# Two transformer blocks in fp32 on one core: sums ahead of the modulation, tables in two loads, reordered gates, half-column sums, compression in four column groups

## The chip, the cores and the metric

One core of one Trainium2 chip runs the whole program. The metric is the device time of one execution in microseconds (us), taken as the median of the runs. Engines: TensorE (PE for matmuls, PEld for its weight loads), VectorE (DVE), ScalarE (ACT), GpSimd (POOL), SyncE (SP, which here only issues transfers).

## What is computed

A sequence of 256 tokens with 1024 features passes through a first block of two layers and a second block of two layers, all in fp32. The reference, cut to what the change touches:

```python
c_act = silu(c)
for i in range(2):                              # first block
    mods = (c_act @ ada_w[i] + ada_b[i])        # 9 x 1024: shift, scale, gate for three sublayers
    h = rmsnorm(x) * (1 + scale) + shift;  x = x + 0.5 * gate * swiglu(h)
    h = ...;                               x = x + gate * (mla, then rwkv7)(h)
    h = ...;                               x = x + 0.5 * gate * swiglu(h)
x = rmsnorm(x)
# second block, layer 0: mixer_ab (dilated attention | convolution + mlstm), layer norm, MoE, layer norm
#   mlstm: gates i, f from the input projection; log_sigmoid(f), cumulative sums, stabilised exponentials
# layer 1: mixer_c, layer norm, MoE, layer norm
def compress(t, pos, w1, w2):                   # 15 windows of 32 tokens, two groups: 30 rows of 4096
    flat = (t[:, cidx] + pos).reshape(..., 32 * 128)
    return gelu(flat @ w1) @ w2                 # w1: 4096 x 256
```

## The kernel before

Activations lie transposed (`xT`: 128 partitions x 8 tiles x 256 tokens). The phases run in the order `ffn0, mla, ffn1, ffn2, rwkv, ffn3, final, ab, moe0, c, moe1`. Each engine has one hand-written instruction list, and semaphores tie the lists together. What an engine does in what order is thus fixed by the place of the call in its own list.

Weights come through a ring of four slots of 2 MB (`ring`), which SyncE fills in the order of `STREAM`; a load waits until the piece four places earlier is given back (`freed`: by VectorE's `dve_free` for modulation and feed-forward pieces, by `slot_free` or `mh_used` for others). In the feed-forwards and the projections of `mla`, `ab` and `c`, a weight is split into a rounded high part (ScalarE: `up_high`, `mix_high`) and a low rest (VectorE: `up_low`, `mix_low`), and each product is three matmuls. `mix_high(g)` and `mix_low(g)` work on half pieces; in `ab` the halves 4 and 5 are the first piece after the two raw ones, 14 to 17 the output weights, in `c` 10 to 13 are the output weights.

**The modulation** (`ada`): 36 pieces of 512 columns. For one piece VectorE multiplies the eight row tiles of the weight by the eight columns of `cact` and adds them up in a chain (`ada_step`, L1876 and L1879, buffer `z` in `work`); TensorE then sums over the partitions with four matmuls whose weights are 128 columns of `z` and whose moving operand is one column of ones (`ada_sum`, L568); VectorE adds the bias into `mods` (`ada_finish`, L1895). Pieces 0 to 3 stand at the very start, before the norm of `ffn0`; the other 32 are spread over the feed-forwards (12, 8, 10, 2), in `ADA_STEPS`. In `ffn0` the norm follows: squares by ScalarE (L1418), column sums by TensorE (`norm_sums`, L548), the root (L1420), the reciprocal (L1943), the scaled tiles (L1953), their high and low parts (L1440, L1950). `hold(6, 7)` issues seven matmuls without use (L541) ahead of the first dense ones, and `up_low` (L1915) must be done for the first tile (L585 are the products).

**Tables.** ScalarE's queue loads at the start `vec`, the whole of `const` (128 x 4673 columns: identity, ones, masks, rotations and so on) and `xT` (L1369 to L1371); TensorE, VectorE and ScalarE wait for `const_in`.

**Mixer `ab`.** TensorE projects with split halves in the order of pieces 3, 4, 5, 6, 0, 1, 2 (`split_piece` L655, `split_tokens` L668), with the two gate columns between them (`by_token`, L1068). VectorE runs low parts, the convolution (`conv`, L2354 and L2356), the gates (L2365, L2366, which TensorE awaits as `lin_fed` for the cumulative sums at L1090), the stabilised exponentials and the normalisation of the linear part, then two low parts, the addition of the mask to the bias table (L2458) and the attention (`maxima` L2088, first thing of each head). The bias table is written to DRAM and read back by ScalarE's queue (`load_bias`, L1638).

**Mixer `c`.** The compression on TensorE (L1323): for keys and for values 32 matmuls over 32 token offsets, weights 128 x 30 (the 30 window rows), moving 128 x 256, all accumulated in 30 partitions of one bank; every fp32 matmul shows as two instructions. ScalarE copies the 30 rows (L1826), TensorE turns them (L1330), ScalarE applies gelu (L1832), TensorE multiplies by `w2`, ScalarE copies (L1835, L1836), and the attention starts. The copies of halves 10 and 11 stand in ScalarE's list between its two copies of raw rows.

## Time and profile before

| | us |
|---|---|
| median of 3 runs (lowest, highest) | 2578.42 (2578.35, 2588.62) |
| profiled execution, own time | 2581.79 |
| its span, first to last instruction | 2580.0 |
| PE busy | 2429.1 (94%) |
| DVE busy | 1709.2 (66%) |
| ACT busy | 1101.5 (43%) |
| POOL busy | 81.4 (3%) |
| mean granted clock of TensorE | 0.964 of 2.4 GHz |

Busy shares are means over phases of different kinds. The chain of waits follows the program back from its last instruction and tells which engine the end hangs on at each time; the timeline gives each instruction with the idle time before it and what ended that. A matmul's own duration includes its way through the array, so rates of matmuls are read from the distance of starts, or from the length of a group divided by its count. "PEclk" is the granted clock: 1.00 is 2.4 GHz, 0.50 is 1.2 GHz.

### The profile page before, as it was taken

To read this page: it belongs to the slowest core of one execution; us is meant where nothing else is said; L and a number is where in the kernel's file an instruction comes from. 1 tells how busy PE (TensorE), PEld (TensorE's weight loads), DVE (VectorE), ACT (ScalarE), POOL (GpSimd) and SP (SyncE) were. 2 spreads that over 40 slices of the span, in tenths; PEclk is the share of its full clock that TensorE was granted. 3 is DMA by queue.
4 is the path that set the end of the run, shared out by engine and by line. 5 is a ranking of instruction groups with operands and counts; after the bars stand their busy time and mean duration, and the time that the engine had idled before them with its cause. 6 is when DMAs were issued, how large, how long until landed. Compare 5 with 4: busy or idle time off the path is not lost.

```text
span 2580.0 us, 40749 instructions
## 1 busy us (share of the span) xinstructions
PE 2429.1 (94%) x17382; PEld 2136.8 (83%) x17382; DVE 1709.2 (66%) x2365; ACT 1101.5 (43%) x1375; POOL 81.4 (3%) x116
## 2 busy tenths in 40 slices
PE   3999989999999998889999989999999989999998
PEld 3999748999999777779999868788888858788886
DVE  5987566876886455655555665548895375557985
ACT  2333254334333033433334443447774252546773
POOL 0000000000000003630000000000000000000000
PEclk9999989999999998889999978999999989999999
DMA  7887304774876230004554503549984400747991
GB/s 294 326 312 270 123 25 158 288 282 154 310 285 256 98 123 26 3 2 185 201 194 124 180 26 126 227 171 354 367 324 185 169 35 21 290 188 304 368 362 49
DMA packets 48284, 502.10 MB, mean 195 GB/s; under 512 B 4968, under 2 KB 9448, under 8 KB 10856
## 3 DMA queue, kind: packets, MB, share of 16 engines
q1 hardware_dynamic: 42480, 490.52, 50.2%
q10 hardware_dynamic: 5624, 8.97, 1.4%
q8 instruction: 138, 2.26, 0.3%
q14 instruction: 42, 0.34, 0.1%
HBM read 496.33 MB, written 3.15 MB: 194 GB/s over the span
## 4 chain that ended last, share of the span: by engine, by line
PE 82%; DVE 11%; ACT 3%; DMA 2%; issue 2%; POOL 1%; ACTq 0%; DVEq 0%; POOLq 0%
PE PS L1229 25%; PE PS L585 25%; PE PS L655 7%; PE PS L631 4%; PE PS L548 2%; DMA ring<-stream 1%; PE PS L668 1%; PE PS L1323 1%; PE PS L568 1%; DVE work L1879 1%; DMA xT<-x_in 1%; PE PS L964 1%; PE PS L767 1%; PE PS L1280 1%; DVE w_up_lo L1915 1%
## 5 line engine op out<-in xcount | busy, mean ns | idle before, releaser
L585 PE MATMUL PS<-x_part_hi,w_up_hi 128*128 128x256 f32 x1408 | 404.4, 287 | 9.4 <-DVE x_part_lo L1950 6.5
L585 PE MATMUL PS<-x_part_lo,w_up_hi 128*128 128x256 f32 x1408 | 399.4, 284 | 0.0
L585 PE MATMUL PS<-x_part_hi,w_up_lo 128*128 128x256 f32 x1408 | 399.3, 284 | 0.0
L2489 DVE TENSOR_TENSOR ring_low<-ring,m_w_up 128x2048 fp32r<-128x2048 f32 x128 | 293.1, 2291 | 134.0 <-ACT m_w_up L1727 134.0
L1727 ACT ACTIVATE m_w_up<-ring 128x2048 fp32r<-128x2048 f32 x128 | 245.3, 1917 | 187.5 <-PE PS L1229 187.5
L585 PEld LDWEIGHTS PS<-x_part_hi,w_up_hi 128*128 128x128 f32 x1408 | 271.0, 193 | 12.7 <-issue 8.0
L585 PEld LDWEIGHTS PS<-x_part_lo,w_up_hi 128*128 128x128 f32 x1408 | 271.3, 193 | 0.0
L585 PEld LDWEIGHTS PS<-x_part_hi,w_up_lo 128*128 128x128 f32 x1408 | 271.1, 193 | 0.0
L1229 PE MATMUL PS<-m_w_up,xg_hi 128*128 128x512 f32 x640 | 253.0, 395 | 3.8 <-DVE work L2503 3.8
L1229 PE MATMUL PS<-ring_low,xg_hi 128*128 128x512 f32 x640 | 254.2, 397 | 0.0
L1229 PE MATMUL PS<-m_w_up,xg_lo 128*128 128x512 f32 x640 | 253.2, 396 | 0.0
L1915 DVE TENSOR_TENSOR w_up_lo<-ring,w_up_hi 128x2048 fp32r<-128x2048 f32 x88 | 201.3, 2289 | 17.7 <-ACT w_up_hi L1386 17.5
L585 PE MATMUL PS<-hid_hi,w_down_hi 128*128 128x256 f32 x704 | 199.3, 283 | 0.0
L585 PE MATMUL PS<-hid_lo,w_down_hi 128*128 128x256 f32 x704 | 199.2, 283 | 0.0
L585 PE MATMUL PS<-hid_hi,w_down_lo 128*128 128x256 f32 x704 | 199.2, 283 | 0.0
L1879 DVE SCALAR_TENSOR_TENSOR work<-ring,cact,work 128x512 f32<-128x512 f32 x252 | 189.0, 750 | 6.9
L1455 ACT ACTIVATE w_down_hi<-ring 128x1024 fp32r<-128x1024 f32 x88 | 93.1, 1058 | 199.6 <-PE PS L585 199.6
L1386 ACT ACTIVATE w_up_hi<-ring 128x2048 fp32r<-128x2048 f32 x88 | 167.1, 1902 | 12.5 <-DMA ring<-stream 12.5
L1229 PEld LDWEIGHTS PS<-m_w_up,xg_hi 128*128 128x128 f32 x640 | 121.0, 189 | 32.7 <-DVE work L2503 4.7
L2047 DVE TENSOR_TENSOR w_down_lo<-ring,w_down_hi 128x1024 fp32r<-128x1024 f32 x88 | 107.5, 1221 | 59.3 <-ACT w_down_hi L1455 58.2
L1450 ACT ACTIVATE work<-PS 128x256 f32<-128x256 f32 x88 | 33.8, 384 | 262.3 <-PE PS L585 262.2
L1229 PEld LDWEIGHTS PS<-m_w_up,xg_lo 128*128 128x128 f32 x640 | 121.0, 189 | 28.6
(523 smaller groups left out, 5158.8 us busy)
## 6 DMA issues: line engine op xcount, KB each, us to landing
ring<-stream SPq DMA_DIRECT2D x133, 2048.0 KB, 7.8
ring<-stream SPq DMA_DIRECT2D x88, 1536.0 KB, 6.7
work<-stream SPq DMA_DIRECT2D x48, 1024.0 KB, 8.3
hT<-stream SPq DMA_DIRECT2D x16, 1024.0 KB, 7.5
ring<-stream SPq DMA_DIRECT2D x3, 1152.0 KB, 5.6
const<-const_tables ACTq DMA_DIRECT2D x1, 2336.5 KB, 18.7
bias_scratch<-work ACTq DMA_DIRECT2D x1, 2048.0 KB
work<-bias_scratch ACTq DMA_DIRECT2D x2, 1024.0 KB, 7.5
```

The lines of the kernel that those rows point to most:

```text
L548: last = mm(bank(7, T, at), ones, ap, start=(i == 0), stop=(i == len(parts) - 1))
L585: last = mm(out, w[a][:, lo:lo + P], x[b][:, at:at + T], start=start and i == 0, stop=stop and i == 2, skip_group_check=skip)
L631: last = mm(bank(m // 2, T, (m % 2) * T, 0, rows), piece_cols(name, k, lo + j * P, rows, width), rhs[:, k, :], start=(k == 0), stop=(k == ...
L655: last = mm(bank(m // 2, T, (m % 2) * T, 0, rows), w[a][:, k, j * step:(j + 1) * step], x[b][:, k * T:(k + 1) * T], start=first[j] and (pa ...
L1229: last = mm(out, x[b], w[a], start=start and i == 0, stop=stop and i == 2)
L1386: fn(w_up[j % 2][0][:, :], piece(f"{tag}.{j}")[:, 0:2048], ACT.Copy).then_inc(S("up_rounded"), 1)
L1455: fn(w_down[j % 2][0][:, :], piece(f"{tag}.{j}")[:, 2048:3072], ACT.Copy).then_inc(S("down_rounded"), 1)
L1727: fn(m_w_up[g % 3][:, :], piece(f"mu{l}.{q}")[:, h * 2048:(h + 1) * 2048], ACT.Copy).then_inc(S("up_rounded"), 1)
L1879: ins = stt(z, w, cact[:, k:k + 1], z, ALU.mult, ALU.add)
L1915: tt_(lo[:, :], piece(f"{tag}.{j}")[:, 0:2048], hi[:, :].bitcast(F32), ALU.subtract).then_inc(S("up_split"), 1)
L2047: tt_(lo[:, :], piece(f"{tag}.{j}")[:, 2048:3072], hi[:, :].bitcast(F32), ALU.subtract).then_inc(dve_free, 1)
L2489: tt_(ring_low[n][:, part], ring[n][:, part], m_w_up[g % 3][:, :].bitcast(F32), ALU.subtract).then_inc(S("up_split"), 1)
```

## The change

1. Head. `norm_sums` now comes before the modulation on TensorE, and VectorE takes the reciprocal between pieces 2 and 3. For pieces 0 to 3, two of the eight row tiles (`ADA_DIRECT = 2`) are multiplied by TensorE straight from the ring (eight matmuls with one moving column), and VectorE's chain has six steps instead of eight; both go into one sum. VectorE gives piece p's slot back only when it has done piece p+1's steps and read piece p's result. `up_low` of tile 0 moves behind the third scaled tile.
2. Tables. `const` is loaded as 264 columns at the start (identity, ones, eps) and the other 4409 in ScalarE's list at tile 6 of `ffn0`; `mla` and GpSimd's `rwkv` wait for that.
3. Modulation sums of the 32 later pieces by halves: each of four matmuls becomes two with 64-column weights, whose results go to partitions 0 to 63 and 64 to 127.
4. `ab`: VectorE's order of low parts 4 and 5, gates and convolution; the bias load, its mask addition and low part 14 earlier, low part 15 inside the attention.
5. `c`: the matmul of offset i goes to the 32-partition group i mod 4, with 32 weight columns (two of them foreign); the copy takes 128 partitions; the turning is a matmul with a folding matrix (four stacked identities) that also adds the four groups. ScalarE's copy of half 11 moves behind the gelu.

```diff
@@ constants and the second load
+CONST_HEAD = 2 * P + 8
-            act.dma_start(const[:, :], const_d[:, :]).then_inc(S("const_in"), 16)
+            act.dma_start(const[:, 0:CONST_HEAD], const_d[:, 0:CONST_HEAD]).then_inc(S("const_in"), 16)
...
                 for j in range(n + 1):
+                    if tag == "ffn0" and j == 6:
+                        act.dma_start(const[:, CONST_HEAD:], const_d[:, CONST_HEAD:]).then_inc(S("const_in"), 16)
@@ ada_sum on TensorE
                 for m in range(4):
-                    last = mm(bank(b + p % 2, 4)[:, m:m + 1], z[:, m * P:(m + 1) * P], ones[:, 0:1], start=True,
-                              stop=True)
+                    for lo in (0, 64):
+                        last = mm(bank(b + p % 2, 4, 0, lo, lo + 64)[:, m:m + 1], z[:, m * P + lo:m * P + lo + 64],
+                                  ones[:, 0:1], start=True, stop=True)
@@ TensorE, pieces 0 to 3, now behind norm_sums("ffn0")
+            def ada_head():
+                pe.wait_ge(S("cact_ready"), 1)
+                for p in range(ADA_HEAD):
+                    take(f"ada.{p}")
+                    if p >= 2:
+                        pe.wait_ge(S("ada_read"), p - 1)
+                    out = bank(4 + p % 2, 4)
+                    for k in range(KT - ADA_DIRECT, KT):
+                        for m in range(4):
+                            mm(out[:, m:m + 1], piece_cols(f"ada.{p}", k, m * P, P), cact[:, k:k + 1],
+                               start=(k == KT - ADA_DIRECT and m == 0), stop=False, skip_group_check=True)
+                    pe.wait_ge(S("ada_part"), p + 1)
+                    z = W(SW_ADA + 512 * (p % ADA_BUFS), 512)
+                    for m in range(4):
+                        last = mm(out[:, m:m + 1], z[:, m * P:(m + 1) * P], ones[:, 0:1], start=False, stop=True,
+                                  skip_group_check=True)
+                    last.then_inc(S("ada_sum"), 1)
+                pe.wait_ge(S("ada_read"), ADA_HEAD)
@@ VectorE, pieces 0 to 3
+            def ada_head():
+                for p in range(ADA_HEAD):
+                    for k in range(KT - ADA_DIRECT):
+                        ada_step(p, k)
+                    if p > 0:
+                        ada_finish(p - 1)
+                        dve.sem_inc(dve_free, 1)
+                    if p == 2:
+                        dve.wait_ge(S("const_in"), 32)
+                        line.next("std_ready")
+                        done(v.reciprocal(RSTD, STD))
+                ada_finish(ADA_HEAD - 1)
+                dve.sem_inc(dve_free, 1)
@@ ab on VectorE
-                dve.wait_ge(S("ab_copied"), 1)
-                mix_lows("ab", 4, 5)
-                conv(0, 4)
+                mix_lows("ab", 4)
                 line.next("softlog_ready")
...
                 done(tt_(lf, lf, sl[:, :, 4:8], ALU.subtract), "lin_fed")
+                mix_lows("ab", 5)
+                dve.wait_ge(S("ab_copied"), 1)
+                conv(0, 4)
...
                 hh = ls(4352, 1024)
+                dve.wait_ge(S("bias_in"), 32)
+                bm = W(A_BM, 8 * ATT).rearrange("p (h c) -> p h c", c=ATT)
+                done(tt_(bm, bm, C("dilated").unsqueeze(1).broadcast_to([P, 8, ATT]), ALU.add))
+                mix_lows("ab", 14)
                 line.next("lnum_copied")
...
-                mix_lows("ab", 14, 15)
-                dve.wait_ge(S("bias_in"), 32)
-                bm = W(A_BM, 8 * ATT).rearrange("p (h c) -> p h c", c=ATT)
-                done(tt_(bm, bm, C("dilated").unsqueeze(1).broadcast_to([P, 8, ATT]), ALU.add))
-                attention("ab", {4: [linear_out], 5: [lambda: mix_lows("ab", 16)], 6: [linear_low]})
+                attention("ab", {4: [linear_out], 5: [lambda: mix_lows("ab", 16)], 6: [linear_low], 2: [lambda: mix_lows("ab", 15)]})
@@ ab on ScalarE: the bias load now behind the copies of halves 10 and 11
                 mix_highs("ab", 10, 11)
+                act.wait_ge(S("bias_stored"), 16)
+                load_bias(A_BM)
@@ c on TensorE
-                            last = mm(bank(4 + 2 * kv, T, T, 0, 2 * NCMP), b3[:, 16 * half + i, :],
-                                      piece(name)[:, i * T:(i + 1) * T], start=(half == 0 and i == 0),
-                                      stop=(half == 1 and i == 15))
+                            at, lo = 2 * NCMP * (16 * half + i), 32 * (i % 4)
+                            n = 32 if at + 32 <= 960 else 2 * NCMP
+                            last = mm(bank(4 + 2 * kv, T, T, lo, lo + n), b3[:, at:at + n],
+                                      piece(name)[:, i * T:(i + 1) * T], start=(half == 0 and i < 4),
+                                      stop=(half == 1 and i >= 12), skip_group_check=True)
...
-                        last = nc.tensor.transpose(bank(4 + 2 * kv + m, 2 * NCMP),
-                                                   W(C_RAW + kv * T + m * P, P, 0, 2 * NCMP),
-                                                   ident[0:2 * NCMP, 0:2 * NCMP])
+                        last = mm(bank(4 + 2 * kv + m, 2 * NCMP), W(C_RAW + kv * T + m * P, P), W(C_FOLD, 2 * NCMP),
+                                  start=True, stop=True)
@@ c on ScalarE
                     if kv == 0:
-                        mix_highs("c", 10, 11)
+                        mix_highs("c", 10)
...
                 last.then_inc(S("hid_gelu"), 1)
+                mix_highs("c", 11)
```

How the instructions stand now. First, the start of TensorE's list: the sums of squares (`hT`), the modulation's matmuls and the warm-up (`const` alone). Before:

```order
L568 MATMUL PS<-const,work 128x1 x16
L548 MATMUL PS<-hT,const 128x256 x8
L541 MATMUL PS<-const 128x256 x7
L585 MATMUL PS<-x_part_hi,w_up_hi 128x256
L585 MATMUL PS<-x_part_lo,w_up_hi 128x256
```

Now:

```order
L551 MATMUL PS<-hT,const 128x256 x8
L586 MATMUL PS<-cact,ring 128x1 x8
L591 MATMUL PS<-const,work 128x1 x4
L586 MATMUL PS<-cact,ring 128x1 x8
L591 MATMUL PS<-const,work 128x1 x4
L586 MATMUL PS<-cact,ring 128x1 x8
L591 MATMUL PS<-const,work 128x1 x4
L586 MATMUL PS<-cact,ring 128x1 x8
L591 MATMUL PS<-const,work 128x1 x4
L544 MATMUL PS<-const 128x256 x7
```

The sums stand first, each piece has twelve narrow matmuls instead of four, and only the warm-up is left between the last of them and the dense ones.

Second, VectorE in `ab` around the gates (two rows of 128x8, L2365 and L2366 before, L2397 and L2398 now; `ring_low` rows are low parts, the 128x256 rows the convolution). Before:

```order
L1922 TENSOR_TENSOR ring_low_49<-ring,half_high_87 128x8x256
L1922 TENSOR_TENSOR ring_low_49<-ring,down_low_85 128x8x256
L2354 TENSOR_SCALAR work<-work,vec 128x256 x4
L2356 SCALAR_TENSOR_TENSOR work<-work,vec 128x256 x12
L2365 TENSOR_SCALAR work<-work 128x8
L2366 TENSOR_TENSOR work<-work 128x8
```

Now:

```order
L1955 TENSOR_TENSOR ring_low_49<-ring,half_high_87 128x8x256
L2397 TENSOR_SCALAR work<-work 128x8
L2398 TENSOR_TENSOR work<-work 128x8
L1955 TENSOR_TENSOR ring_low_49<-ring,down_low_85 128x8x256
L2388 TENSOR_SCALAR work<-work,vec 128x256 x4
L2390 SCALAR_TENSOR_TENSOR work<-work,vec 128x256 x12
```

The gates no longer stand behind one low part and half of the convolution.

Third, VectorE at the end of the linear part of `ab`, before the first head of the attention (L2088 before, L2122 now, 128x384). Before:

```order
L2442 TENSOR_TENSOR work<-work 128x1024
L1922 TENSOR_TENSOR ring_low_50<-ring,down_low_85 128x8x256
L1922 TENSOR_TENSOR ring_low_50<-ring,half_high_86 128x8x256
L2458 TENSOR_TENSOR work<-work,const 128x3072
L2088 SCALAR_TENSOR_TENSOR work<-PS,work 128x384
```

Now, the two places to which they moved, with the rows between left out:

```order
L2448 TENSOR_REDUCE work<-work 128x8
L2452 TENSOR_TENSOR work<-work,const 128x3072
L1955 TENSOR_TENSOR ring_low_50<-ring,down_low_85 128x8x256
L2456 TENSOR_SCALAR work<-work 128x8
...
L2481 TENSOR_TENSOR work<-work 128x1024
L2122 SCALAR_TENSOR_TENSOR work<-PS,work 128x384
```

The mask addition and one low part now precede the wait for the linear numerator (L2456), and the attention follows the linear part directly; the other low part stands after the third head's scores.

## Rows read from the trace of the kernel before

**Rows 1.** The page, part 4: shares of the span in the chain of waits.
```profile
PE 82%; DVE 11%; ACT 3%; DMA 2%; issue 2%; POOL 1%; ACTq 0%; DVEq 0%; POOLq 0%
```

**Rows 2.** Timeline, 0 to 56 us: start us, us, engine, line, operation, [idle before <-releaser].
```profile
10.26 5.47 DVE L1879 SCALAR_TENSOR_TENSOR work<-ring,cact,work 128x512 f32<-128x512 f32 x7
...
27.29 3.57 PE L568 MATMUL PS<-const,work 128*128 128x1 f32 x16 [27.29 <-DMA xT<-x_in]
...
43.64 5.66 PE L548 MATMUL PS<-hT,const 128*128 128x256 f32 x16 [0.25 <-DVE mods L1895]
...
49.14 3.19 PE L541 MATMUL PS<-const 128*128 128x256 f32 x14
...
49.92 1.75 DVE L1943 RECIPROCAL small<-small 128x256 f32<-128x256 f32 x1 [6.14 <-ACT small L1420]
...
55.61 0.55 PE L585 MATMUL PS<-x_part_hi,w_up_hi 128*128 128x256 f32 x1 [3.29 <-DVE x_part_lo L1950]
```

**Rows 3.** TensorE's waits in the `ab` mixer, 1383 to 1570 us: total, times, longest.
```profile
PE PS L701 <- DVE work L2090: 8.8, 1, 8.8
...
PE PS L1090 <- DVE work L2366: 5.4, 1, 5.4
```

**Rows 4.** Timeline of the `c` mixer, 2036 to 2092 us, three engines.
```profile
2041.24 29.35 PE L1323 MATMUL PS<-ring,work 128*30 128x256 f32 x128
...
2064.34 3.71 ACT L1395 ACTIVATE half_high<-ring 128x2048 fp32r<-128x2048 f32 x2 [7.15 <-DMA ring<-stream]
...
2070.63 0.37 ACT L1826 ACTIVATE work<-PS 30x256 f32<-30x256 f32 x1 [2.58 <-PE PS L1323]
...
2076.06 0.19 DVE L2088 SCALAR_TENSOR_TENSOR work<-PS,work 128x30 f32<-128x30 f32 x1 [5.19 <-PE PS L699]
```

**Rows 5.** Windows: us, length, busy (count) of PE, PEld, DVE, ACT, POOL, PEclk, DMA, GB/s.
```profile
20.00:25.00 5.00, 0.00 (x0) 0.00 (x0) 4.75 (x8) 0.00 (x0) 0.00 (x0) 1.00 0.99 421
55.00:60.00 5.00, 4.39 (x20) 4.42 (x21) 5.00 (x13) 3.03 (x7) 0.00 (x0) 0.50 0.01 3
100.00:110.00 10.00, 10.00 (x86) 10.00 (x85) 9.42 (x15) 3.36 (x3) 0.00 (x0) 1.00 0.89 335
```

**Rows 6.** DMA issues: KB each, median us from issue to landing.
```profile
ring<-stream SPq DMA_DIRECT2D x88, 1536.0 KB, 6.7
...
const<-const_tables ACTq DMA_DIRECT2D x1, 2336.5 KB, 18.7
...
xT<-x_in ACTq DMA_DIRECT2D x1, 1024.0 KB, 25.6
```

**Rows 7.** The chain of waits in order of time, 0 to 130 us.
```profile
101.38 0.79 PE PS L568 x8
```

**Rows 8.** TensorE's timeline behind a dense stretch of the `ab` mixer.
```profile
1406.60 1.85 PE L1068 MATMUL PS<-ring,xT 128*128 128x8 f32 x16
...
1408.69 2.86 PE L1068 MATMUL PS<-ring,xT 128*128 128x8 f32 x16
```

**Rows 9.** ScalarE's timeline in the first feed-forward.
```profile
104.92 1.92 ACT L1386 ACTIVATE w_up_hi<-ring 128x2048 fp32r<-128x2048 f32 x1 [2.45 <-DMA ring<-stream]
```

**Rows 10.** TensorE's timeline in the `rwkv` mixer: matmuls with 64-column weights.
```profile
1021.91 1.15 PE L981 MATMUL PS<-work 128*64 128x64 f32 x32
...
1024.76 0.39 PE L1017 MATMUL PS<-work 128*64 128x128 f32 x4
...
1024.98 0.39 PE L1021 MATMUL PS<-work 128*64 128x128 f32 x4
```

**Rows 11.** VectorE's timeline in the `ab` mixer, 1418 to 1512 us.
```profile
1421.92 2.29 DVE L1922 TENSOR_TENSOR ring_low<-ring,down_low 128x2048 fp32r<-128x2048 f32 x1 [9.87 <-ACT down_low L1395]
...
1490.36 0.17 DVE L2417 TENSOR_SCALAR work<-work 128x8 f32<-128x8 f32 x1 [4.33 <-ACT work L1700]
...
1506.07 3.35 DVE L2458 TENSOR_TENSOR work<-work,const 128x3072 f32<-128x3072 f32 x1
...
1509.45 0.56 DVE L2088 SCALAR_TENSOR_TENSOR work<-PS,work 128x384 f32<-128x384 f32 x1
```

62 lines of the change are left out of this document (30 added, 32 removed).

## Prediction

> **What bounds the kernel now.** The chain of waits comes first: TensorE carries 82% of it and VectorE 11% [rows 1], so a change pays only where TensorE stands still, runs at half clock, or does fewer cycles. The timeline then shows three such places. At the head, TensorE does its first matmul at 27.29 us and its first dense product at 55.61 [rows 2]; between them lie the modulation's four pieces (each seven chained VectorE steps, 5.47 us, after a first one), the sums of squares (5.66), a warm-up (3.19) and the reciprocal (1.75). In the `ab` mixer TensorE's waits name two stops on VectorE, 5.4 and 8.8 us [rows 3]. In the `c` mixer one line of 128 half-instructions takes 29.35 us with weights of 30 columns [rows 4]. Elsewhere dense products follow each other, and only fewer or cheaper instructions count there.
>
> **Head: what the new order gives.** All early loads share the engines: 421 GB/s at 20 to 25 us [rows 5]. The tables and x go out from ScalarE's queue and land 18.7 and 25.6 us after issue [rows 6], x at 27.3. The table load shrinks from 2336 KB to 132, so 2.26 MB less lie ahead of x: at 421 GB/s that is 5.4 us, x lands at 21.9. ScalarE squares it, and the sums start at 22.9 and end at 28.6 (5.66 us, partly cold [rows 2]). Piece 0 on TensorE is now 8 narrow products straight from the weights and 4 from VectorE's partial sum, 24 instructions where there were 8. Cold, 16 took 3.57 us, 0.22 each [rows 2]; warm, 8 took 0.79, 0.10 each [rows 7]. After a dense stretch 16 narrow ones still took 1.85 us (warm) and only the next 16 2.86 [rows 8], so piece 0 is warm: 2.4 us, until 31.0. VectorE has by then done pieces 0 and 1 (six steps of 0.78, 4.7 us, instead of eight) and stands at piece 0's result; this is a new wait, and the loads behind it wait too, since the ring's first slot is now given back at 31.2, not near 16. Then piece 2 until 35.7, result and reciprocal until 37.5, piece 3 until 42.2. TensorE has done piece 3's direct part by then; the last four products, cold, take 1.8: 44.0. The old order had the modulation at 43.6, so nothing is won up to here. What is won stands behind it: sums, root, reciprocal and the first weight subtraction no longer follow. Fourteen warm-up matmuls from cold take 5.2 us (5.66 less two warm ones of 0.23 [rows 2]) and hide the subtraction: dense work starts at 49.3, not 55.6, and warm, where it ran at a clock of 0.50 before [rows 5]. VectorE's eight scaled tiles and the second subtraction then hold TensorE's second tile until 56.1 where it was 63.1. Gain **7.0 us**. The first two weight pieces, requested at 31.2 and 35.8, land 6.7 us later [rows 6] and are rounded by 44.4, just in time; the ring is full at about 54, and its next slot comes free only at 58.5. If TensorE is cold for all of it, 4 us come back; if x lands early enough for VectorE alone to set the pace, 4 more are won: 3 to 11.
>
> **The rest of the tables** (2.26 MB) now goes out in the first feed-forward after tile 5. There transfers are busy for 0.89 of the time at 335 GB/s [rows 5], and ScalarE already waits 2.45 us for a piece [rows 9] while TensorE never idles. At that rate the load takes 6.7 us and shares the engines with the pieces. The wait shown says that the margin is small. Bounds: nothing if the free tenth and the ring's stock absorb it, 6.7 if nothing does. I take **+3.0**.
>
> **Modulation sums by halves.** Behind the head 32 pieces pay 0.79 us each [rows 7] on the chain. Now a set is 16 instructions with 64-column weights, in alternating halves. The nearest row: 32 instructions with 64-column weights and 64 columns moving took 1.15 us, 0.036 each [rows 10], so a set takes 0.58, 0.21 less; 32 of them 6.7. Twelve lie in the first feed-forward, where data is short, and count half: **5.5 us**. Bounds: 0.025 each (a quarter of the 0.10, full overlap) gives 10; 0.05 each (half of it, no overlap) gives nothing, and a little lost at each switch +2.
>
> **The gates' order in `ab`.** VectorE does the two small gate operations before the convolution and a weight subtraction (2.29 [rows 11]), so TensorE's wait of 5.4 us goes. With it goes the cold stretch behind it, worth 2.7 us (dense products at half speed for some 5.4 us, as begins at 55.61 [rows 5]): 8.1 in all. What is late next is the 8.8 us wait. VectorE's bias addition (3.35) and two subtractions stand ahead of its first score at 1509.45, starting at 1501.7: 7.8 us that go. The addition and one subtraction (5.6) move up to where VectorE idled 4.33 us [rows 11]; the bias load moves up on ScalarE's queue and should land before. That costs 1.7. The other subtraction (2.2) goes into the attention, in which VectorE sets the pace. Sum: 8.1 + 7.8 - 1.7 - 2.2 = **12.0 us**; 9 if upstream gains are partly covered by the wait for weights, 14.5 if the shorter stop keeps the clock up.
>
> **Compression in four groups.** The 128 instructions take 0.229 each with 256 columns moving [rows 4]. Now neighbours write four different 32-row groups. That groups overlap is in the trace: with two 64-column groups 4 instructions of 128 columns start every 0.22 us, 0.055 each [rows 10], half of 128 x 0.229/256 = 0.115. I take full overlap, 0.057. The first two weight pieces then take 5.1 us (cold for the first 3) instead of 14.6. But ScalarE's half of the output weights stands between the two results and needs a slot that the second piece frees: before, freed at 2055.9 (half of the 29.35 behind 2041.24) and landed at 2064.3 [rows 4], 8.4 us; now freed at 2046.3, landed at 2054.7. One copy (1.86), then the second result at 2056.6, where before it was 2070.6. From there 5.5 us to VectorE's first score, plus 0.7 because copy and subtraction of half 11 now lie behind it: 2062.8, not 2076.06. Gain **13.3 us**, not the 22 that TensorE alone would save: the rest turns into a wait on that transfer. The four copies that build the folding matrix and the folding itself (8 instructions for 4) cost under 0.5 us in VectorE's idle time and in the 5.5. Bounds: 15 if the transfer is faster, 9.6 if only two groups overlap, -1 if none.
>
> A rule speaks against this part. In the Trainium skill, "TensorE: Matmul & The Clock Gate", section "The mechanism", a weight load overlaps with running matmuls only when the row group differs; here all groups use all 128 rows. By the letter of it the four groups would be serial, which is the first rival. The trace disagrees for two groups (0.055 against 0.115), so I follow the trace.
>
> **Sum.** -7.0 + 3.0 - 5.5 - 12.0 - 13.3 = -34.8 us. The profiled execution took 2581.8 us, so 2547.0 for it; the median of the runs lies 3.4 lower, at 2578.4, and so does the forecast: **2543.6 us**. A measurement of this kernel can tell some 0.5%, 13 us, from no change.
>
> **Rivals.**
> A, the column groups are serial: the compression gives -1 instead of 13.3, 2543.6 + 14.3 = 2557.9. For it: no row has four groups. Against: [rows 10]. 8%.
> B, the first feed-forward is bound by its transfers: the second table load costs its 6.7 (3.7 more than summed) and the halves' gain in that stage is lost (1.3): 2548.6, and with the head's gain lost too, because slots came free 15 us later, 2555.6. For it [rows 5, 9]; against, the transfers stood idle at 55 to 60 us (3 GB/s, [rows 5]), so stock is not short there. 10%.
> C, TensorE stays cold through the whole head, 24 instructions of 0.22 for piece 0 and sums that take 1.1 longer: 4 us, 2547.6. 8%, inside the range.
> D, slower: the narrow half-column sets cost the clock. If the granted clock fell to 1.2 GHz behind each of the 32 sets, the dense products after it would lose 2.7 us each, as behind a stop now: 86 us. With the halves' 5.5 gone, -29.3 + 86 = +57, 2635. It decides from 11 sets on (29.3/2.7). For it: narrow matmuls did lower the clock in [rows 8]. Against: that took over 3 us of them, these sets last under 1 us, and behind today's sets the clock stays at 1.00 [rows 5]. 2%.
> E, the edits do their parts but new waits eat most of it (the bias load late, or VectorE late in `ab`): 2560 to 2580. 3%.
> The forecast itself has 69%.
>
> **Numbers.** The range is 2532 to 2557: the good ends of two or three terms on one side, B and C whole on the other; A, D and E stay out. Faster by over 0.5% (under 2565.5) 0.94, within 0.5% 0.04, slower 0.02.
>
> **What would show it.** Head: VectorE idle some 11 us before its first result, first dense product at 49 to 50 us. Tables: ScalarE waits for pieces right behind the load. Sets of 16 in under 0.6 us. In `ab`, no wait of TensorE for the gates, and its last one under 3 us. In `c`, TensorE done with the compression near 2050 on the old scale and ScalarE waiting for a transfer before the second result. It is wrong if the first dense product comes after 54 us, if the compression's instructions start 0.2 us apart, or if a clock of 0.50 shows in the feed-forwards.

## The result, and the profile after

The changed kernel takes 2546.57 us (median of 4 runs, 2541.78 to 2549.04) against 2578.66 for the kernel before (4 runs on the same chip, 2578.35 to 2588.62). The ratio is 0.9864, with a 95% interval of 0.9836 to 0.9892: 32.1 us less, where the prediction had 34.8, and its 2543.6 us is 3.0 below the median. The pair of profiled executions differs by more, 2581.79 to 2541.78 or 40.0 us. The lengths of the stages show where.

The page of the changed kernel, parts 1, 4 and 5 (line engine op, out<-in, shapes, count | busy, mean ns | idle before, releaser). L604 was L585 before, L1409 was L1386, L1948 was L1915:

```profile
PE 2406.5 (95%) x17706; PEld 2121.7 (84%) x17706; DVE 1703.5 (67%) x2361; ACT 1101.2 (43%) x1375; POOL 81.3 (3%) x116
...
PE 78%; DVE 12%; DMA 4%; ACT 3%; issue 2%; POOL 1%; ACTq 0%; DVEq 0%; POOLq 0%
...
L604 PE MATMUL PS<-x_part_hi,w_up_hi 128*128 128x256 f32 x1408 | 404.2, 287 | 8.9 <-DVE w_up_lo L1948 5.4
...
L1409 ACT ACTIVATE w_up_hi<-ring 128x2048 fp32r<-128x2048 f32 x88 | 167.3, 1903 | 34.9 <-DMA ring<-stream 34.7
```

TensorE's share of the chain fell from 82% [rows 1] to 78%, and transfers doubled theirs to 4%. ScalarE's waits for ring pieces grew from 12.5 us to 34.7: the kernel now waits for data where it waited for arithmetic.

The norm's sums (L551, L548 before) open every stage, and the chain of waits gives their times. Their starts in the changed kernel, behind the head's own:

```profile
257.16 3.71 PE PS L551 x16
411.35 3.47 PE PS L551 x16
617.56 3.71 PE PS L551 x16
824.65 3.47 PE PS L551 x16
1173.89 3.64 PE PS L551 x16
1375.53 3.69 PE PS L551 x16
1535.94 3.47 PE PS L551 x16
...
1934.50 3.47 PE PS L551 x16
...
2120.32 3.47 PE PS L551 x16
...
2518.67 3.47 PE PS L551 x16
```

The differences of neighbours are the stages' lengths; the same view of the kernel before gives the other column. "Predicted" sorts the prediction's terms by stage (12 of the 32 sets lie in the first feed-forward, 20 in the others).

| stage | before | after | gain | predicted |
|---|---|---|---|---|
| head and first feed-forward | 261.48 | 257.16 | 4.3 | 5.3 |
| `mla` | 155.73 | 154.19 | 1.5 | 0 |
| other three feed-forwards | 616.97 | 614.94 | 2.0 | 4.2 |
| `rwkv` | 350.77 | 349.24 | 1.5 | 0 |
| `ab` | 176.52 | 160.41 | 16.1 | 12.0 |
| `moe0` | 403.39 | 398.56 | 4.8 | 0 |
| `c` | 195.30 | 185.82 | 9.5 | 13.3 |
| `moe1` | 398.54 | 398.35 | 0.2 | 0 |

Four stages that no edit reaches gained 8.1 us. `moe0` shows what that is. In 14 profiled executions of 14 programs it took 398.4 to 404.9 us although its instructions never changed, and the other stages scatter likewise. This is the row of its first stretch in the kernel before, and then in the changed one (us, length, busy of PE, PEld, DVE, ACT, POOL with counts, granted clock, DMA share, GB/s):

```profile
1561.50:1624.00 62.50, 56.48 (x274) 47.76 (x273) 42.14 (x93) 27.32 (x33) 0.00 (x0) 0.86 0.47 188
```

```profile
1536.00:1595.60 59.60, 53.32 (x274) 44.83 (x272) 42.09 (x93) 27.30 (x33) 0.00 (x0) 0.91 0.50 198
```

The same 274 matmuls take 2.9 us more at a mean granted clock of 0.86 than at 0.91. Across the 14 executions `moe0`'s mean granted clock is 0.99 in the shortest and 0.97 in the longest. Such episodes of the lower level (1.2 instead of 2.4 GHz) differ between executions, and they can account for a profiled pair that differs by 40 where the medians differ by 32. Stage lengths are therefore compared only where an edit acts and where rows inside show the cause.

**The head** (TensorE, VectorE, ScalarE's rounding copies and the sync queue, changed kernel; "..." marks rows left out):

```profile
22.91 6.29 PE L551 MATMUL PS<-hT,const 128*128 128x256 f32 x16 [22.91 <-ACT hT L1441]
...
29.03 1.84 PE L586 MATMUL PS<-cact,ring 128*128 128x1 f32 x16
...
31.68 3.56 PE L586 MATMUL PS<-cact,ring 128*128 128x1 f32 x16
31.93 0.16 DVE L1920 TENSOR_TENSOR mods<-PS,vec 128x4 f32<-128x4 f32 x1 [12.96 <-PE PS L591]
32.00 15.60 SPq L482 DMA_DIRECT2D ring<-stream  x4
...
38.36 1.91 ACT L1409 ACTIVATE w_up_hi<-ring 128x2048 fp32r<-128x2048 f32 x1 [8.66 <-DMA ring<-stream]
...
47.22 0.16 DVE L1920 TENSOR_TENSOR mods<-PS,vec 128x4 f32<-128x4 f32 x1 [3.56 <-PE PS L591]
47.43 5.55 PE L544 MATMUL PS<-const 128*128 128x256 f32 x14 [0.25 <-DVE mods L1920]
...
56.70 2.29 DVE L1948 TENSOR_TENSOR w_up_lo<-ring,w_up_hi 128x2048 fp32r<-128x2048 f32 x1
```

The sums start at 22.91 (predicted 22.9), and VectorE idles 12.96 us before its first result ("some 11"). The first slot comes free at 32.00. Piece 0's 16 narrow instructions take 1.84 us; from piece 1 on 16 take 3.56: the clock had fallen. With the 8 instructions of the partial sum that is 5.1 us a piece, more than the 4.6 that VectorE needs for six steps and a result. The modulation is done at 47.4 instead of 44.0, and the first dense product comes at 52.6 instead of 49.3.

**`ab`.** The chain's fourth block of input products, in the kernel before and in the changed one:

```profile
1447.28 11.36 PE PS L655 x96
```

```profile
1429.52 11.35 PE PS L674 x96
```

Counted from the stage's first sums (1384.95 and 1375.53) it starts at 62.33 and 53.99, 8.3 us earlier. TensorE's waits of 5.4 and 8.8 us [rows 3] are both gone from its list; the longest left are 1.8 and 2.8, both inside the attention (at 1485.9 and 1493.4). VectorE's small gate operation now stands at 1406.26, the bias addition (3.36) at 1468.30, and the first score is read at:

```profile
1406.26 0.17 DVE L2398 TENSOR_TENSOR work<-work 128x8 f32<-128x8 f32 x1
...
1484.67 0.56 DVE L2122 SCALAR_TENSOR_TENSOR work<-PS,work 128x384 f32<-128x384 f32 x1
```

**`c`.** TensorE, ScalarE and VectorE, changed kernel:

```profile
2011.58 6.91 PE L1344 MATMUL PS<-ring,work 128*32 128x256 f32 x96
...
2020.83 3.00 PE L1344 MATMUL PS<-ring,work 128*32 128x256 f32 x32 [2.35 <-DMA ring<-stream]
2027.64 1.91 ACT L1418 ACTIVATE half_high<-ring 128x2048 fp32r<-128x2048 f32 x1 [10.42 <-DMA ring<-stream]
2029.46 0.36 ACT L1851 ACTIVATE work<-PS 128x256 f32<-128x256 f32 x1
...
2036.19 0.19 DVE L2122 SCALAR_TENSOR_TENSOR work<-PS,work 128x30 f32<-128x30 f32 x1 [0.48 <-PE PS L718]
```

What took 29.35 us [rows 4] takes 12.2, of which 2.35 are a wait for the fourth weight piece. The transfer for ScalarE's half lands at 2027.64 and holds the second result until 2029.46, as foretold.

### The profile page after: what moved, and what is told of

Its sections match the earlier page's. It is cut to its first block, busy times and chain, and to the rows that moved or that the text cites. A ratio compares the mean times of both kernels' runs of the same rounds, so it can differ in the third digit from the quotient of the medians.

```text
span 2540.0 us, 41400 instructions
## 1 busy us (share of the span) xinstructions
PE 2406.5 (95%) x17706; PEld 2121.7 (84%) x17706; DVE 1703.5 (67%) x2361; ACT 1101.2 (43%) x1375; POOL 81.3 (3%) x116
## 4 chain that ended last, share of the span: by engine, by line
PE 78%; DVE 12%; DMA 4%; ACT 3%; issue 2%; POOL 1%; ACTq 0%; DVEq 0%; POOLq 0%
PE PS L1248 25%; PE PS L604 23%; PE PS L674 7%; PE PS L650 4%; DMA ring<-stream 3%; PE PS L551 2%; DVE work L1908 1%; PE PS L983 1%; PE PS L687 1%; DVE w_up_lo L1948 1%; PE PS L786 1%; DMA xT<-x_in 1%; PE PS L1299 1%; PE PS L748 1%; PE PS L992 1%
## 5 line engine op out<-in xcount | busy, mean ns | idle before, releaser
L604 PE MATMUL PS<-x_part_hi,w_up_hi 128*128 128x256 f32 x1408 | 404.2, 287 | 8.9 <-DVE w_up_lo L1948 5.4
L604 PE MATMUL PS<-x_part_hi,w_up_lo 128*128 128x256 f32 x1408 | 398.3, 283 | 0.0
L604 PE MATMUL PS<-x_part_lo,w_up_hi 128*128 128x256 f32 x1408 | 398.2, 283 | 0.0
L604 PEld LDWEIGHTS PS<-x_part_hi,w_up_hi 128*128 128x128 f32 x1408 | 269.6, 191 | 12.9 <-DVE w_up_lo L1948 7.7
L604 PEld LDWEIGHTS PS<-x_part_lo,w_up_hi 128*128 128x128 f32 x1408 | 269.9, 192 | 0.0
L604 PEld LDWEIGHTS PS<-x_part_hi,w_up_lo 128*128 128x128 f32 x1408 | 269.9, 192 | 0.0
L1948 DVE TENSOR_TENSOR w_up_lo<-ring,w_up_hi 128x2048 fp32r<-128x2048 f32 x88 | 201.2, 2288 | 19.0 <-ACT w_up_hi L1409 18.9
L604 PE MATMUL PS<-hid_hi,w_down_hi 128*128 128x256 f32 x704 | 199.3, 283 | 0.0
L604 PE MATMUL PS<-hid_lo,w_down_hi 128*128 128x256 f32 x704 | 199.2, 283 | 0.0
L604 PE MATMUL PS<-hid_hi,w_down_lo 128*128 128x256 f32 x704 | 199.1, 283 | 0.0
L1908 DVE SCALAR_TENSOR_TENSOR work<-ring,cact,work 128x512 f32<-128x512 f32 x244 | 183.0, 750 | 6.6
L1409 ACT ACTIVATE w_up_hi<-ring 128x2048 fp32r<-128x2048 f32 x88 | 167.3, 1903 | 34.9 <-DMA ring<-stream 34.7
L1248 PEld LDWEIGHTS PS<-ring_low,xg_hi 128*128 128x128 f32 x640 | 120.1, 188 | 27.3
```

The source lines that it names most:

```text
L604: last = mm(out, w[a][:, lo:lo + P], x[b][:, at:at + T], start=start and i == 0, stop=stop and i == 2, skip_group_check=skip)
L1248: last = mm(out, x[b], w[a], start=start and i == 0, stop=stop and i == 2)
L1409: fn(w_up[j % 2][0][:, :], piece(f"{tag}.{j}")[:, 0:2048], ACT.Copy).then_inc(S("up_rounded"), 1)
L1908: ins = stt(z, w, cact[:, k:k + 1], z, ALU.mult, ALU.add)
L1948: tt_(lo[:, :], piece(f"{tag}.{j}")[:, 0:2048], hi[:, :].bitcast(F32), ALU.subtract).then_inc(S("up_split"), 1)
```

## The experiments

Each is the changed kernel with one edit, or with several where the text says so; "+" and "-" are against it, and "..." marks what is left out. Ratios are to the kernel before, timed beside it. The runs come from several chips, so two experiments are compared by their ratios and intervals first. Lengths of stages are from one profiled execution each.

**Full-width sets.**

```diff
-  for lo in (0, 64):
-      last = mm(bank(.., lo, lo + 64)[:, m:m + 1], z[:, m * P + lo:m * P + lo + 64], ones[:, 0:1], ...)
+  last = mm(bank(b + p % 2, 4)[:, m:m + 1], z[:, m * P:(m + 1) * P], ones[:, 0:1], ...)
```

> The changed kernel with its 32 modulation sums behind the head at full width again (8 instructions a set). Theory of the prediction: a set costs 0.79 us instead of 0.58, so the second to fourth feed-forward (20 sets) end 4.2 us later against the stage before, and the run is 5.5 us slower than the changed kernel. Rival, from the changed kernel's trace, where those three stages gained 2.0 us in all: the switch of column groups takes half of it back, 0.10 us a set, so 2.0 us there and 3 in all. In the first feed-forward nothing, if transfers bound it.

Measured: 2553.64 us, ratio 0.9900 [0.9877, 0.9922]. The chain of waits in the second feed-forward repeats a double tile with one set. This kernel:

```profile
494.37 17.38 PE PS L603 x144
512.54 17.38 PE PS L603 x144
```

and the changed one:

```profile
489.21 17.46 PE PS L604 x144
507.24 17.46 PE PS L604 x144
```

The period is 18.17 and 18.03: 0.14 us a set, between the two theories. The set itself shrank by 0.22 (18.17 - 17.38 = 0.79, 18.03 - 17.46 = 0.57), as the prediction had it, but 0.08 comes back in the dense products around it: the first narrow instruction starts 0.21 us behind the last dense one, whose neighbours start 0.12 apart (a full-width set follows after 0.12 too). Over 32 sets 4.5 us. The medians differ by 7.1, but stages without a set scatter by more than the rest: `moe1` took 405.0 us in this profiled execution and 398.4 in the changed kernel's. A property listed in the Trainium skill, "TensorEngine Tiling (Array Packing)", section "Key Properties", says that changing the tiling mode drains the engine; the extra 0.09 us fits that, though no run here separates a drain from another cause.

**Half-column sets, one group after the other.**

```diff
-  for m in range(4):
-      for lo in (0, 64):
+  for lo in (0, 64):
+      for m in range(4):
```

> The changed kernel with the 16 half-column instructions of each modulation set in another order: first the four of rows 0 to 63, then the four of rows 64 to 127, instead of alternating. In the changed kernel a set takes 0.56 us (0.035 each) and the double tile of the feed-forward with its set 18.03 us, against 18.17 with full-width sets. Theory: what makes a half-column instruction cheap is that its weight load runs beside the other column group's work, so with one switch in place of seven a set costs 0.8 us or more and the period is 18.2 or more. Rival: the price is that of the 64 columns alone (half the weights to load), order does not matter, and the period stays at 18.03.

Measured: 2557.88 us, ratio 0.9901 [0.9881, 0.9920]. Its chain:

```profile
473.99 17.46 PE PS L604 x144
492.27 17.46 PE PS L604 x144
```

Period 18.28, set 0.82 us: slower than full width. The theory holds: the alternation makes the halves cheap, not their width.

**The rest of the tables at tile 18.**

```diff
-  if tag == "ffn0" and j == 6:
+  if tag == "ffn0" and j == 18:
```

> The changed kernel with the second table load (2.2 MB) sent after tile 18 of the first feed-forward instead of tile 6, where no modulation piece is loaded any more. If the load costs what the prediction says, the end of the first feed-forward comes 3.0 us earlier (6.7 if it costs its whole transfer) and the long waits for ring pieces at 103 and 121 us shrink. Rival: the stage is short of data already because the first four slots come free late, the stall only moves to another piece, and the end moves by under 1 us.

Measured: 2547.84 us, ratio 0.9883 [0.9860, 0.9907], and the stage ended at 260.07, later than the 257.16 it should have beaten. Neither theory held. The head shows something else: the program is the same there, yet here piece 1's narrow products ran at the full clock too:

```profile
28.29 1.84 PE L586 MATMUL PS<-cact,ring 128*128 128x1 f32 x16
30.00 1.03 PE L591 MATMUL PS<-const,work 128*128 128x1 f32 x8
30.89 1.93 PE L586 MATMUL PS<-cact,ring 128*128 128x1 f32 x16
31.14 0.16 DVE L1920 TENSOR_TENSOR mods<-PS,vec 128x4 f32<-128x4 f32 x1 [12.26 <-PE PS L591]
```

The modulation was done at 44.3 and the first dense product came at 49.12, the prediction's own 44.0 and 49.3. In all eight executions with this order of the head piece 0 was warm and pieces 2 and 3 were cold. Piece 1 was warm in four of them (first dense product at 49.1 to 49.9) and cold in four (52.5 to 52.9). The windows from 32 to 34 us of the changed kernel and of the experiment on output halves below, which run the same program up to here:

```profile
32.00:34.00 2.00, 2.00 (x11) 2.00 (x11) 1.93 (x4) 0.00 (x0) 0.00 (x0) 0.50 0.60 111
```

```profile
32.00:34.00 2.00, 2.00 (x20) 2.00 (x20) 1.93 (x3) 0.00 (x0) 0.00 (x0) 1.00 0.81 190
```

Estimated from such rows, the clock fell at 31.2 to 32.0 us in the four late executions and at 32.8 to 34.0 in the four early ones. The Trainium skill, "TensorE: Matmul & The Clock Gate", section "What's actually happening", says that the count of cold matmuls at a kernel's start varies from run to run; these runs agree, with 3 us. Little of the 3 us reached the end of the stage: the four early executions ended it at 257.5 to 260.1, the four late ones at 257.2 to 262.0. TensorE's wait for weights in this stage came to 8.2 us here, and to 3.4 in the changed kernel (total, times, longest):

```profile
PE PS L604 <- DVE w_up_lo L1948: 8.2, 7, 2.2
```

```profile
PE PS L604 <- DVE w_up_lo L1948: 3.4, 4, 1.7
```

**The rest of the tables behind x.**

```diff
   act.dma_start(xT[:, :], x_d[:, :]).then_inc(S("const_in"), 16)
+  act.dma_start(const[:, CONST_HEAD:], const_d[:, CONST_HEAD:])...
...
-  if tag == "ffn0" and j == 6:
-      act.dma_start(const[:, CONST_HEAD:], ...)
```

> The changed kernel with the rest of the tables (2.2 MB) sent right behind x instead of in the first feed-forward after tile 6. Transfers stand idle between 22 us (x and the first four pieces have landed) and 32 us (the first slot comes free), so theory: the load is free there, x still lands at 22, the waits for ring pieces at 103 and 121 us (13.5 and 8.9 us of the chain) shrink to some 7 each, and the first feed-forward ends 3 to 6 us earlier than at 257.2, near 252.5. Rival: the load shares the engines with x and the pieces from the start, x lands 3 to 5 us later (25 to 27), and the head gives back what the stage wins: end at 255 to 258. Second rival, from the run with the tables at tile 18, whose stage ended 2.9 us later: the stage's stalls come from the four slots and not from the tables, and the end moves by under 1 us.

Measured: 2542.49 us, ratio 0.9864 [0.9834, 0.9895]. The sums start at 22.64, so x isn't held back, and between 22 and 30 us 437 GB/s move where the changed kernel moved 193:

```profile
22.00:30.00 8.00, 7.36 (x37) 6.50 (x37) 0.00 (x0) 2.52 (x5) 0.00 (x0) 1.00 1.03 437
```

The load is free there, and still the stage ends at 257.48: the second rival. TensorE waits 5.6 us for weights without the 2.2 MB in the stage; with them it waited 3.4, 5.2, 5.4 and 7.7 us in four executions.

**No direct products in the head.**

```diff
-ADA_DIRECT = 2
+ADA_DIRECT = 0
```

> The changed kernel without direct products in the head: VectorE does all eight steps of each piece, TensorE 4 sums. If the cold narrow products of TensorE set the pace of the head (5.12 us a piece in the changed kernel), VectorE's 5.9 us a piece for the pieces 2 and 3 now does: piece 1's result at 29.9, modulation done near 44.5 to 46 where it was 47.2, so the head is 1 to 3 us faster although VectorE does more. Rival: VectorE set the pace, and two more steps on two pieces make it 3 us slower (50).

Measured: the modulation was done at 45.8, within the theory, so TensorE indeed set the pace of the changed head; the stage ended at 254.46. But the four runs spread from 2547.76 to 2557.66, median 2553.40, ratio 0.9906 [0.9880, 0.9931], slower than the changed kernel if anything. The profiled execution is the fastest of the four, and what held the others isn't in a trace. This stays open.

**Slots given back early.** Pieces 0 and 1 wholly on VectorE, pieces 2 and 3 as they were.

```diff
-ADA_DIRECT = 2
+ADA_DIRECT = (0, 0, 2, 2)
...
-  if p >= ADA_HEAD:
+  if p >= ADA_HEAD or ADA_DIRECT[p] == 0:
       dve.sem_inc(dve_free, 1)
```

> The changed kernel, but VectorE does all eight steps of pieces 0 and 1 and gives their ring slots back right behind them, as the kernel before did; pieces 2 and 3 keep their direct products. Theory from nine traces: behind the head the first feed-forward is bound by the four ring slots and ends 225 to 229 us after the first slot comes free (changed kernel: free at 32.0, end at 257.2), wherever the tables go and wherever the first dense product starts. Here the first slots come free near 15.6 and 21.5 and the first dense product stays at 51 to 53: the end must then be set by computing, 201 us behind the first dense product as in the run with both head edits, near 253, with under 1.5 us of TensorE waits for weights in the stage. Rival: the third and fourth slot decide, and the end stays at 256 to 258.

Measured: 2545.18 us, ratio 0.9866 [0.9832, 0.9899]. The first slot came free at 15.66, the first weight piece was rounded at 30.36 instead of 38.36, and the stage ended at 252.92 as expected. By another sum, though: the first dense product came at 47.69 and not at 51 to 53, and the end not 201 behind it but 205.2, with 4.1 us of waits for weights and not under 1.5. The earlier dense product isn't owed to the slots: with no direct products for pieces 0 and 1 the first result was read at 29.30 and the modulation was done at 42.3, and the warm-up follows that. What the slots gave is less clear. The waits of 4.1 us are below the 5.1 to 8.2 of the four executions with a dense start at 49.1 to 49.9, but in the range of all eight, and waits for ring pieces remain at 70, 94 and 116 us of the chain. "The end is 226 behind the first slot" is thus refuted as a rule (237 here).

**Pieces 0 and 1 ahead of the norm's sums.**

```diff
+  pe.wait_ge(S("cact_ready"), 1)
+  ada_head(0, 2)
   norm_sums(ph)
-  ada_head()
+  ada_head(2, ADA_HEAD)
```

> The changed kernel with the products of pieces 0 and 1 ahead of the norm's sums on TensorE (it stands idle until x lands at 22), and the reciprocal behind piece 3's steps on VectorE. If what holds the head is VectorE idle for 13 us behind piece 0's result, the modulation is done near 35 us instead of 47.2 and the first dense product starts near 41 instead of 52.6. If the first feed-forward were bound by computing, all 11 to 12 us would reach its end. Theory now: the stage is bound by its transfers behind the head (ring pieces waited for at 75, 103, 121, 149 us), and since slots come free 11 us earlier, the transfers start earlier too: 5 to 10 us at its end. Rival: the engines that move data are full anyway until 130 us, and under 3 us reach the end.

Measured: 2534.40 us, ratio 0.9830 [0.9807, 0.9854]. The median is 12 us under the changed kernel's and the ratio 0.34% lower (9 us), with intervals that overlap. The modulation is done at 40.3, the first dense product comes at 45.65, the stage ends at 250.49: 6.7 of the 7.0 us reach its end, inside the 5 to 10. This head also gives the first slot back at 23.84 instead of 32.00, so the run doesn't separate slots from the earlier dense start. The modulation came late against the hoped 35, because its input now waited for the small tables until 14.56. Another 4.6 us are `rwkv`'s (344.65 instead of 349.24), a stage no edit touches, at a higher granted clock; the runs don't show that they belong to this edit.

**More of the same.** Added to the kernel just told: the small tables on a semaphore of their own, the rest of the tables behind x as above, and the first weight subtraction ahead of the last result.

```diff
-  act.dma_start(const[:, 0:CONST_HEAD], ...).then_inc(S("vec_in"), 16)
+  act.dma_start(const[:, 0:CONST_HEAD], ...).then_inc(S("bias_stored"), 16)
...
+  up_low("ffn0", 0)
   ada_finish(ADA_HEAD - 1)
```

> The kernel with pieces 0 and 1 ahead of the norm's sums, and in addition: the modulation vector no longer waits for the small tables (they held it until 14.6 instead of 9.4), the rest of the tables goes out behind x, and the first weight subtraction stands ahead of VectorE's last modulation result instead of behind it. Theory: modulation done near 35 us instead of 40.3, first dense product near 40.5 instead of 45.7 (the 14 warm-up matmuls now set it), the end of the first feed-forward near 244 instead of 250.5. Rival: transfers hold x back (25 instead of 22), or the stage is bound by its slots and the end moves by under 3 us.

Measured: 2535.57 us, ratio 0.9837 [0.9804, 0.9869]. The stage ended at 249.00 where 244 was expected and 250.49 stood before, so the end moved by under 3 us, as the rival had it. But x wasn't held back, as that rival had it: it landed at 22.0. The sums start at 24.20 because ScalarE now loads its activation table (1.28 us) behind x, and so it does in the last experiment below, whose tables go out at tile 6. What came late is piece 3, at 31.96 (26.78 in that last experiment), and with it the modulation, at 41.3. The slots are free from 19.0 on, so the tables go out beside new pieces, and their load took 30.0 us where it took 12.8 in the last experiment:

```profile
31.96 0.48 DVE L1908 TENSOR_SCALAR work<-ring,cact 128x512 f32<-128x512 f32 x1 [5.56 <-DMA ring<-stream]
```

Dense work began 28 us behind the first slot, TensorE's waits for weights fell to 1.2 us, and the end came 201.7 behind the first dense product.

**Gate operations behind the convolution again.**

```diff
-  done(ts_(lf, ...)); done(tt_(lf, ...), "lin_fed")
   mix_lows("ab", 5)
   dve.wait_ge(S("ab_copied"), 1)
   conv(0, 4)
+  done(ts_(lf, ...)); done(tt_(lf, ...), "lin_fed")
```

> The changed kernel with the two small gate operations of the ab mixer behind the convolution again. The two traces put 8.3 us on this part (from the stage's norm sums to the fourth pair of product blocks). If the two small operations alone do that, TensorE waits 5.4 us for VectorE again, the blocks behind it run cold for 2.7 us, and the stage is 8.3 us longer (168.7 instead of 160.4). Rival: the bias addition that now stands in VectorE's idle time absorbs part of the delay, so 5.4 to 6.

Measured: 2560.62 us, ratio 0.9908 [0.9876, 0.9941]; `ab` took 169.83, 9.4 more than 160.41. The first score, counted from the stage's start, comes 8.5 us later, and the wait is back, as the expectation had it:

```profile
PE PS L1109 <- DVE work L2400: 5.4, 1, 5.4
```

**Compression in two groups.**

```diff
-  at, lo = 2 * NCMP * (16 * half + i), 32 * (i % 4)
+  at, lo = 2 * NCMP * (16 * half + i), 64 * (i % 2)
```

> The changed kernel with the compression's products in two groups of rows (0 and 64) instead of four; the folding matrix and the unused rows are zeroed. In one group an instruction took 0.229 us, in four 0.054. If the groups stream side by side, two give half of the serial time, 0.115 each, the first pair of weight pieces takes 7.4 us instead of 5.2, the slot for the output weights comes free 2.5 us later and the second result and the stage end that much later (c stage 188 instead of 185.6). Rival: what overlaps is the weight load alone, and two alternating groups already hide it: 0.054 to 0.06 each and no difference in the stage.

Measured: 2548.70 us (2 runs), ratio 0.9870 [0.9831, 0.9910]; `c` took 188.61, 2.8 more. The weight loads behind the cold start, here and then in the changed kernel:

```profile
2018.43 12.26 PEld L1344 LDWEIGHTS PS<-ring,work 128*32 128x32 f32 x114 [0.24 <-issue]
```

```profile
2014.57 3.44 PEld L1344 LDWEIGHTS PS<-ring,work 128*32 128x32 f32 x64 [0.23 <-issue]
```

One group, in the kernel before, at the same place:

```profile
2044.23 25.88 PEld L1323 LDWEIGHTS PS<-ring,work 128*30 128x30 f32 x120 [0.25 <-issue]
```

That is 12.26/114 = 0.108 us and 3.44/64 = 0.054 each, and 25.88/120 = 0.216 in one group (0.229 with the cold start). Groups stream side by side, and the price halves with each doubling of their number. The stage's 2.8 us are not the products' alone: ScalarE copies each result here in two parts, 0.76 us instead of 0.38.

**Output halves out of the compression.**

```diff
-      if kv == 0:
-          mix_highs("c", 10)
...
-  mix_highs("c", 11)
...
-  attention("c", {6: [lambda: mix_highs("c", 12)]})
+  attention("c", {2: [.. 10], 4: [.. 11], 6: [.. 12]})
```

> The changed kernel with ScalarE's two halves of the c mixer's first output weights taken out from between the compression's results and put into the attention (halves 10 and 11 at its steps 2 and 4, the subtractions at 3 and 5). Theory: the compression on TensorE is done at 2023.9, and only the wait for the transfer that lands at 2027.6 and one copy hold its second result until 2029.5, another copy of 1.9 stands behind it: the second result then comes 5.5 us earlier and the first score 7 us earlier; in the attention VectorE has two more subtractions of 2.3, so 2.5 to 7 us less for the c stage (185.6). In the ab attention one such subtraction cost nothing. Rival: VectorE sets the pace of the attention and the two subtractions cost more there than they gain (over 7 us), or the bias additions on VectorE end later than the second result and hold the first score: under 1 us.

Measured: 2548.81 us, 2537.10 to 2554.70, ratio 0.9862 [0.9825, 0.9899]: no difference that the medians show. In the trace `c` took 182.33, 3.5 less. The compression started at 2020.8, 9.2 later than in the changed kernel, because stages before it were longer:

```profile
2033.59 0.38 ACT L1851 ACTIVATE work<-PS 128x256 f32<-128x256 f32 x1 [7.12 <-PE PS L1344]
...
2039.17 0.19 DVE L2120 SCALAR_TENSOR_TENSOR work<-PS,work 128x30 f32<-128x30 f32 x1 [29.79 <-PE PS L718]
```

So the second result came 5.1 us earlier (2029.46 + 9.2 - 2033.59) and the first score 6.2. From the first score to the output product 61.92 us became 64.99: the attention gave 3.1 back. Beside it, this run shows the first feed-forward again: dense from 49.43, waits for weights 7.7 us, end at 258.17.

**All that paid together**: head order, own semaphore, the early subtraction, 6 warm-up matmuls, tables at tile 6, output halves in the attention.

```diff
-  hold(6, 7)
+  hold(6, 3 if tag == "ffn0" else 7)
```

> The changed kernel with what the runs pointed to: pieces 0 and 1 ahead of the norm's sums on TensorE, the modulation vector free of the small tables, the rest of the tables again after tile 6 (behind x they delayed x by 1.4 us and piece 3 by some 5), the first weight subtraction ahead of the last modulation result, 6 warm-up matmuls instead of 14 in the first feed-forward, and the c mixer's first output halves inside its attention. Theory: x at 22, first slot free at 19, modulation done at 35 to 37, first dense product near 39 to 41, end of the first feed-forward at 19 + 226 = 245 if the slots bind and 40 + 201 = 241 if computing does, so 245 (257.2 in the changed kernel); c stage 182.3 instead of 185.8. Sum 12 + 3.4 = 15.5 us under the changed kernel's 2546.6: 2531, ratio to before 0.9815. Rival: less warm-up and the earlier start only add stalls with a lower clock behind them, and it stays at the 2534 to 2536 of the runs with the head edits alone.

Measured: 2533.29 us (5 runs, 2531.78 to 2540.99), ratio 0.9817 [0.9788, 0.9845]. It is clear of the kernel before and can't be told from the head edit alone (2534.40, 0.9830); its interval just overlaps the changed kernel's. The modulation is done at 38.5 and dense work starts at 40.96, 11.7 us before the changed kernel's, but the stage ends at 248.88, only 8.3 before, where 245 was expected. Behind the shorter warm-up the first dense products still start 0.21 us apart, until 43.8, and TensorE waits for weights:

```profile
PE PS L604 <- DVE w_up_lo L1952: 4.1, 5, 1.6
```

## Why the prediction was right, and where it wasn't

The time and the sign were right; the terms were so in part, and errors of opposite sign offset each other.

*Head, 7.0.* Transfer and sums came as computed, and VectorE's new wait was 13.0 us for some 11. "Piece 0 is warm" held in all eight executions. The step that failed in half of them is the pace behind it: the prediction let VectorE set it (piece 2 until 35.7, piece 3 until 42.2) and had TensorE's direct part of piece 3 done by then. By the prediction's own price of cold products, 24 of 0.22 us, TensorE needs 5.3 us a piece and VectorE 4.7. Where piece 1 was warm, this didn't show, and dense work began at 49.1 to 49.9 where 49.3 was forecast; where it was cold (5.1 us measured), the first dense product came at 52.5 to 52.9. Rival C priced about that much, 4 us, but by a cold piece 0 that never happened. What the step missed more deeply is what the first dense product is worth. Take the end of the first feed-forward, less the first dense product, less TensorE's waits for weights. In eleven of the 13 kernels that have the new head or a variant of it this is 200.5 to 202.9 us (201.1 in the changed kernel); the other two are full-width sums (204.2) and the shortened warm-up (203.8). So this part is nearly constant, and what an earlier start wins is in part lost again in waits, 1.2 to 8.2 us of them. Rival B was right in that the stage is short of data, behind a first slot freed at 32 instead of 15.8: waits for ring pieces take 15.8% of the chain up to 262 us, 3.4% in the kernel before. It was wrong in its price for the tables, as the next term shows. The argument against it, that transfers "stood idle at 55 to 60 us", was read from the kernel before, whose four slots were full at that time and whose TensorE started dense work at 55.61; it says nothing about a kernel whose slots come free 16 us later. The stage gained 4.3 us in the profiled execution; the three others with the same program up to there ended at 258.2, 260.2 and 260.9, so 0.6 to 4.3 where 5.3 was forecast.

*Tables, +3.0.* The experiment priced it at nothing that can be seen: 257.48 without the load in the stage, 257.16 with it. Even the longest waits, 13.5 us of the chain at 103 us, only moved elsewhere. With late tables the stage was 2.9 longer, with a further wait for a piece in its chain at 213 us.

*Half-column sets, 5.5.* The set is 0.57 us (0.58 forecast). The term missed the 0.08 at the switch, which its bounds had in words ("a little lost at each switch", +2). 0.14 for 20 sets is 2.8; the profiles show 2.0 for those stages against before and 3.8 against full width. The two references, both with full-width sets, differ by 1.7 themselves, so the period is the better measure. Rival D, the clock falling behind each set, didn't happen: the periods are constant to 0.01.

*`ab`, 12.0.* Measured 15.7 up to the output product, in the profiled pair, each point taken from the stage's start. The gate step brought 8.3 (8.1 forecast: 5.4 of wait, 2.7 of cold products) and, put back, cost the wait of 5.4 again and 9.4 in the stage. The bias step brought 7.0 (7.8 - 1.7 = 6.1 forecast). Its cost was 1.3, which is what the prediction's own numbers give (5.6 - 4.33), not the 1.7 that it wrote, and 8.3 went behind it. The step that failed is the last: "the other subtraction (2.2) goes into the attention, in which VectorE sets the pace". From the first score to the output product 28.80 us became 28.46. So VectorE has gaps there that take a subtraction whole; in `c` two of them cost 3.1.

*Compression, 13.3.* Full overlap was right (0.054 against 0.057 each), and so was the transfer as the new bound. Measured from the compression's start, the second result came 11.5 us earlier (14.0 forecast) and the output product 10.2. Mis-sized is the transfer: 8.4 us from slot to landing, as before, were really 10.8. Other loads went out just before and behind it (at 2011.68, 2015.10 and 2018.56, this one at 2016.83), and the engines moved 420 GB/s over the whole 10.8 us; over the 8.4 us before they moved 250. That is 2.4 of the 3.1 us. Rival A (8%) fell: 0.216, 0.108 and 0.054 for one, two and four groups. The rule it stood on, in the Trainium skill, "TensorE: Matmul & The Clock Gate", section "The mechanism", allows a weight load to overlap only across row groups; these rows disagree, and agree with "Tiles operate independently" in "TensorEngine Tiling (Array Packing)", section "Key Properties".

So `ab` gave 3.7 more than forecast, `c` 3.1 less, the head and the feed-forwards 3.2 less (6.3 instead of 9.5, and more in other executions). The sum fits to 3 us because these cancel. That is luck within the bounds, not precision.

## What to carry to other kernels

An earlier start of a stage that lives on a ring of four slots is worth what is left after the waits for data that it brings: price both the first product and these waits. Here neither the start nor the first free slot gave the end by itself. Products that wait only for pieces already loaded go before those that wait for other inputs. Before two engines are given parts of one job, compare their pace per piece at either clock level. In `ab` the waits went by putting the small work that another engine awaits first, and the large work into VectorE's idle time, and a subtraction moved into a phase with gaps may cost nothing, so read the gaps and not only who sets the pace. Where a step's speed hangs on the clock staying up through narrow work, give both courses a real chance: here it was four executions of eight.

## What the runs showed of the hardware

Column groups run side by side: instructions with 30 or 32 weight columns and 256 columns moving cost 0.216 us each in one group, 0.108 in two and 0.054 in four. With 64-column weights the order matters as much as the width: 16 such instructions take 0.57 us alternating between the halves and 0.82 in two blocks of eight, more than eight full-width ones (0.79). The first instruction of such a set starts 0.21 us behind a full-width product, where full-width ones follow each other after 0.12. And the same instructions can take different times in two executions: an unchanged stage of 400 us took 398.4 to 404.9 us in 14 of them, at a mean granted clock of 0.99 in the shortest and 0.97 in the longest.
